# Gated delta stage of a streaming encoder step: front woven into the last gated unit, modulation loads issued after k times state, first-level blocks ahead of the state update

## The reference, cut to what matters

```python
# gated unit: y (tokens x 512) against w_glu (512 x 1024)
za, zb = jnp.split(y @ w_glu, 2, axis=-1)
y_a = za * jax.nn.sigmoid(zb)
# gated delta rule, 4 heads of 128, with the per-head decay and the write strength beta
A = strict_lower((k_beta @ k.T) * dmask);  T = inverse(eye + A)
v_new = u - w @ S                      # u, w = T @ (v_beta, k_beta * exp(decay))
o     = q_dec @ S + (q @ k.T * dmask) @ v_new
S     = S * exp(decay_last) + k_dec.T @ v_new
# modulation: six vectors of 1024 from the conditioning vector; the last four serve later stages
mod = silu(c) @ w_ada + b_ada          # w_ada is 1024 x 6144
```

## Time and profile before

| | us |
|---|---|
| runs of the kernel before (3) | 1420.83, 1422.02, 1426.58 |
| median | 1422.02 |
| the profiled execution: its own time | 1422.2 |
| its span in the trace | 1420.5 |
| gated delta stage in it, 408.7 to 594.1 | 185.4 |
| mean granted TensorE clock (1 is 2.4 GHz) | 0.98 |

### The profile page before, as it was taken

The page is one execution under the profiler, slowest core; times in us unless marked ns, Lnnn a source line. Parts: engine busy times, 40 slices in busy tenths (PEclk is TensorE's granted clock), DMA queues, the critical chain, the costliest instruction groups (busy, mean ns, idle before and its releaser), DMA issues.

```text
span 1420.5 us, 28873 instructions
## 1 busy us (share of the span) xinstructions
PE 1350.5 (95%) x10652; PEld 1237.5 (87%) x10652; DVE 952.9 (67%) x1487; ACT 584.7 (41%) x1331; POOL 547.7 (39%) x618
## 2 busy tenths in 40 slices
PE   5999899989989998899999999999999999999997
PEld 4899899988978887688799999999999997887675
DVE  6527686774367766687879655676666568676398
ACT  6524344436466564425544333333332325543120
POOL 4888866871122322133331434432443431000051
PEclk9999999999989999999999999999999999999999
DMA  9431435335455453432132444554344449996794
GB/s 345 125 103 47 113 94 134 104 88 151 113 179 164 140 177 128 147 116 82 67 105 95 131 162 146 186 186 157 124 160 157 149 153 378 379 332 219 261 328 180
DMA packets 184406, 234.61 MB, mean 165 GB/s; under 512 B 17709, under 2 KB 118641, under 8 KB 184305
## 3 DMA queue, kind: packets, MB, share of 16 engines
q1 hardware_dynamic: 180128, 221.36, 48.2%
q10 hardware_dynamic: 4176, 11.89, 2.2%
HBM read 170.29 MB, written 61.73 MB: 163 GB/s over the span
## 4 chain that ended last, share of the span: by engine, by line
PE 60%; DVE 7%; issue 4%; ACT 3%; POOL 1%; DMA 1%; POOLq 0%; ACTq 0%; DVEq 0%; SPq 0%
PE bank L2461 30%; PE bank L2375 12%; PE bank L308 3%; PE bank L1161 2%; PE bank L1745 2%; PE bank L1177 1%; PE bank L1175 1%; PE bank L2392 1%; ACT hp L1835 1%; DVE stat L1868 1%; PE bank L1225 1%; DVE xt L1903 1%; PE bank L1216 1%; PE bank L1206 1%; PE bank L1218 1%
## 5 line engine op out<-in xcount | busy, mean ns | idle before, releaser
L2375 PE MATMUL bank<-split 128*128 128x512 f32 x924 | 212.4, 390 | 3.3 <-DVE split L2508 3.0
L2375 PEld LDWEIGHTS bank<-split 128*128 128x128 f32 x924 | 172.6, 188 | 45.3 <-DVE split L2504 6.5
L2461 PE MATMUL bank<-Tlo,rh 128*128 128x272 f32 x640 | 184.7, 289 | 0.0
L2461 PE MATMUL bank<-Thi,rh 128*128 128x272 f32 x640 | 184.2, 288 | 0.0
L2461 PE MATMUL bank<-Thi,rl 128*128 128x272 f32 x640 | 184.0, 288 | 0.0
L308 PE MATMUL bank<-hT_hi,whi 128*128 128x384 f32 (+1 forms) x504 | 167.8, 333 | 3.5 <-DVE wlo L298 3.3
L308 PE MATMUL bank<-hT_hi,wlo 128*128 128x384 f32 (+1 forms) x504 | 165.8, 329 | 0.0
L308 PE MATMUL bank<-hT_lo,whi 128*128 128x384 f32 (+1 forms) x504 | 165.7, 329 | 0.0
L2461 PE MATMUL bank<-hT_lo,rh 128*128 128x272 f32 x480 | 138.5, 289 | 0.0
L2461 PE MATMUL bank<-hT_hi,rl 128*128 128x272 f32 x480 | 138.4, 288 | 0.0
L2461 PE MATMUL bank<-hT_hi,rh 128*128 128x272 f32 x480 | 137.9, 287 | 0.0
(11 more groups left out here) (443 smaller groups left out, 3329.8 us busy)
## 6 DMA issues: line engine op xcount, KB each, us to landing
wada<-w_ada SPq DMA_DIRECT2D x12, 2048.0 KB, 9.7
raw<-w_up SPq DMA_DIRECT2D x40, 512.0 KB, 5.0
wsum<-w_down SPq DMA_DIRECT2D x11, 1024.0 KB, 5.6
wt<-wsum SPq DMA_DIRECT2D x11, 1024.0 KB, 4.0
rW<-wt SPq DMA_DIRECT2D x44, 256.0 KB, 6.0
split<-split SPq DMA_DIRECT2D x22, 512.0 KB, 5.0
wraw<-w_in SPq DMA_DIRECT2D x21, 512.0 KB, 4.4
rows<-convrow ACTq DMA_DIRECT2D x16, 577.5 KB, 3.6
```

The lines of the kernel that those rows point to most:

```text
L2375: last = pe.matmul(ps[down_bank(q, r)][:], a[:, rows], w, start=(k == 0 and m == 0), stop=(k == KH - 1 and m == 2))
L2461: last = pe.matmul(ps[banks[c]][:, 0:NC], w[:, ks], a, start=(n < 3 and k == 0 and p == 0), stop=(k == 3 and p == 2), skip_group_check=True)
```

## The change

It has these parts, which all touch the stage's order and no arithmetic.

1. **Front.** The gate half of block 3 leaves `glu_pe` and is made in three pieces (`glu_gate`, banks 3, 4, 2) inside the delta stage's list; the transposes, products and ACT copies of tiles 0 and 1 stand between these pieces and those of the value half. Tile 0 has an Xc buffer of its own (`XcF`).
2. **Modulation loads.** `ada(t+2)` is issued behind k times state of tile t and behind the load of q, k, v, no longer at the end of pass t. `ada(1)` waits for level 4 of tile 0. The halves of the output weights (`wo_load`) move from the ends of passes 6 and 7 to behind k times state of passes 6 and 7.
3. **Modulation products.** `ada_rows` runs one pass earlier: `ada_rows(0)` in the front, `ada_rows(t+1)` at the end of pass t, none in pass 7. `ada_columns(t)` moves from behind `new_values` to ahead of `turn_v`, into free columns of bank 1, and only heads 2 and 3 of `outputs` wait for its reader.
4. **DVE.** `first_level(n)` goes ahead of `new_state(t)`. In pass 8 `wo_low(4)` and `tile_lo(0, 0)` go behind `new_state(8)`.
5. **ACT.** The exponentials of the decay go from behind the rounds to between the second and the third round.

```diff
 (gdn_loads)
             sp.wait_ge(on["glu_mix"], 12)
+            ada(0)
             qkv(2)
-            for t in range(2):
-                ada(t)
...
+            sp.wait_ge(on["g_X"], lvp(0, LV - 2, PAIRS - 1) + 1)
+            ada(1)
             for t in range(TILES):
-                if t == PTILES:
-                    sp.wait_ge(on["ada_mm"], ADA0 + PTILES)
-                    wo_load(1)
+                sp.wait_ge(on["g_kS"], (t + 1) * HEADS)
+                if t + 3 < TILES:
+                    sp.wait_ge(on["g_qd"], t + 1)
+                    qkv(t + 3)
+                if t + 2 < PTILES:
+                    sp.wait_ge(on["ada_mm"], ADA0 + t + 1)
+                    ada(t + 2)
+                if 1 <= t and t + 1 < TILES:
+                    sp.wait_ge(on["g_mix"], t)
+                    z(t + 1)
                 if t + 4 < TILES:
                     sp.wait_ge(on["g_E"], (t + 2) * 3 + 3)
                     decay_rows(t + 4)
...
-                if t == PTILES - 2:
+                if t in (PTILES - 2, PTILES - 1):
                     sp.wait_ge(on["ada_mm"], ADA0 + t + 1)
-                    wo_load(0)
+                    wo_load(t - (PTILES - 2))
 (gdn_pe, front)
+            glu_gate(pe, 0)
+            decay_turn(pe)
+            turn_k(0)
+            pe.wait_ge(on["gate_d"], 3)
+            turn_q(0, ALL)
+            glu_gate(pe, 1)
+            glu_gate(pe, 2)
+            gram(0, 0)
+            gram(0, 1)
             glu_last(pe, 0)
...
+            turn_k(1)
             glu_last(pe, 1)
+            pe.wait_ge(on["gates"], 1)
+            turn_A(0)
             glu_last(pe, 2)
             scores(0)
...
             level_X(0, 2)
+            ada_rows(0)
 (gdn_pe, pass)
                 if t:
                     turn_o(t - 1)
+                if t < PTILES:
+                    ada_columns(t)
                 if more:
                     turn_v(n, ALL)
                 new_values(t)
-                if t:
-                    ada_columns(t - 1)
                 outputs(t, FIRST2)
                 if more:
                     turn_A(n)
                 outputs(t, LAST2)
                 if more:
                     scores(n)
-                if t < PTILES:
-                    ada_rows(t)
+                if t + 1 < PTILES:
+                    ada_rows(t + 1)
 (outputs)
-                pe.wait_ge(on["mod_cols"], ADA0 + t)
+                if heads is LAST2:
+                    pe.wait_ge(on["mod_cols"], ADA0 + min(t + 1, PTILES))
 (gdn_act, pass)
                     if more:
-                        decay_diff(n, FIRST2)
+                        decay_diff(n, ALL)
                     keep_P(t, 4)
                     keep_P(t + 1, 1)
                     if more:
-                        decay_diff(n, LAST2)
+                        decay_exp(n)
+                        decay_row(n)
                     keep_P(t, 5)
                     keep_P(t + 1, 2)
                     whole_X(t)
                     if more:
-                        decay_exp(n)
-                        decay_row(n)
                         squares_k(n)
 (gdn_dve, pass)
-                else:
-                    wo_low(dve, 4)
-                    tile_lo(dve, 0, 0)
+                if more:
+                    first_level(n)
                 new_state(t)
                 if more:
-                    first_level(n)
                     later_levels(n)
...
                 else:
-                    dve.wait_ge(on["mod_st"][0], 32)
...
+                    wo_low(dve, 4)
+                    tile_lo(dve, 0, 0)
                     for k in range(5, KD):
                         wo_low(dve, k)
```

More of the change, by code:

```diff
@@ L946, in glu_act @@
                     gates_exp(act)
+            weights(3)
         def glu_dve(dve):
@@ L1170, in level_X @@
                         if l == LV - 1:
-                            last = pe.matmul(x_at(t, p, UP, i, 1), Pb[x][DOWN, h, 0:HB], Xc[x][DOWN, h, 1, :], start=True, stop=True)
+                            last = pe.matmul(x_at(t, p, UP, i, 1), Pb[x][DOWN, h, 0:HB], Xt(t)[DOWN, h, 1, :], start=True, stop=True)
                             continue
```

254 lines of the change are left out of this document (129 added, 125 removed).

## The result

The changed kernel takes **1402.47 us** (median of 4 runs, 1402.07 to 1403.87). The kernel before, measured beside it, took 1424.3 (4 runs, 1420.83 to 1427.94). The ratio is 0.9848, with a 95% interval from 0.9818 to 0.9878: faster by 1.2 to 1.8%. The profiled execution took 1402.45 with a span of 1400.7; before it was 1422.2 with 1420.5. The two profiles are 19.8 apart, and the sum had 13.2.

What follows compares the result with a forecast made beforehand. PE, busy 95%, bounds the kernel, so gains come from its stalls and waits in the delta stage. Terms -10.0, -3.0, -2.2, +2.1, -0.4, -1.0 and +1.3 sum to -13.2: 1422.2 to 1409.0 us, range 1402 to 1421.

Steps and rivals of the forecast that it cites:

- What bounds the kernel: PE busy 95% of the span; gains must come from its idle or slow time in the delta stage, not removed work.
- Loads: Delta passes 1 to 7: w_ada load moved behind k times state ends instruction-fetch stalls; -10.0 us, bounds 0 and -11.4.
- one stall that survives: Allowance of 1.4 us within the loads' saving, for one instruction-fetch gap remaining in the delta passes.
- The rival that the load is not the cause: PE's stalls in the delta passes have another cause, so the loads' saving falls away; 1419 us, chance 0.15.
- Columns: End of each delta pass: outputs no longer wait for DVE; -0.5 a pass, -3.0 for six, -2.2 for passes 7 and 8.
- First level ahead of the state: DVE at pass ends: state update finishes later and delays the next round; +0.3 a pass, +2.1 for seven passes.
- DVE becomes the bound: Rival: stalls go, but each delta pass pays the late state update and queued DVE work; 1416 us, chance 0.15.
- Exponentials: ACT's decay exponentials move to where ACT waits for PE in the rounds; taken as nothing, bounds -2 and 0.
- ada_rows earlier, passes 7 and 8: Pass 7 loses a 1.92 us PE product, but output-weight splits hold pass 8's first round; -0.4, bounds 0 and -1.9.
- Front: Ahead of pass 1: first coupling ready sooner, mostly given back by ACT's copies and added ada_rows(0); -1.0 us.
- Output projection: Two splits behind the last state update delay PE's first projection matmul by 2.4, partly hidden in idle time; +1.3 us.
- The slower rival: The load reaches the next delta pass's rounds, stalling every pass with lower clock, 3.9 us each; 1435 us, chance 0.07.

## Why the prediction was right, and where its sizes were off

**What bounds the kernel** held: PE's waits and clock in the delta stage, and not its work. The forecast's mechanism is what happened, and the three rivals fell. The number owes something to chance. The profiles are 19.8 apart where 13.2 was forecast, and the time came within 0.5 us of the range's end. Of the 19.8, 3.7 came with the clock in the front of before, and the stages ahead of the front took 1.8 of it back.

**Loads (-10.0 taken, of it -8.7 in passes 1 to 6).** Right in cause, a little small. Moving only the load gave -10.2 in these six passes, the full 10.1 that the bound held. That the fetches wait for the load, which the prediction had only from an overlap in time, is shown by the packets, which start 2.4 to 4.8 us later when the load stands ahead of the rounds. The term that was mis-sized is "one stall that survives", for which 1.4 was left: the one that did measured 0.59, and made its pass 1.0 longer than the gap-free ones beside it (20.50 against 19.53 and 19.52). In pass 7 the gap of 1.34 went as well in the changed kernel, though that pass's load is the output weights and the edit of w_ada alone did not remove it (1.61 there). The change moved the loads of the output weights too, which may be the reason; no run isolates it. The rival that the load is not the cause (1419) fell with both runs of the load. The Trainium skill, "Runtime: NRT & Kernel Launch", section "Instruction fetch mechanics", which stood beside this rival, calls a crossing "one DMA tail-bump, mostly hidden". The packets at 442, 462 and 482 us, met by a full q1 and followed by no gap, are as it says, while those in the rounds of short matmuls cost 0.97 to 1.70 each with the load put back. The rule holds here for the one place and not for the other.

**Columns (-0.5 a pass, between -0.15 and -1.1).** Right: 0.53 a pass by the run that undoes it. The outputs follow the new values after 1.18 (1.2 forecast). Of the 2.2 taken for passes 7 and 8 the half for pass 7 was wrong: with the columns put back that pass is as long (17.17), because its end waits for the state update behind the splits. The half for pass 8 can't be checked alone. With all other terms, the two passes gave -4.2 where -3.6 was forecast.

**First level ahead of the state (+2.1 for seven passes).** Wrong in size: 0.16 in passes 1 and 3, nothing in 2, 4 and 6, hidden in pass 5. The step that failed is the end of the state update, worked out at 536.6, which is 6.75 behind the outputs, where the next round started 6.03 behind them. It ended 6.08 behind them (503.68 against 497.60). The collision with POOL met one operation of the three and made it 1.41 instead of 0.42, so it was paid once and not carried on, and four heads took 1.11 and not 1.22. What was left is hidden where the round begins with the other tile, one in two as the prediction had said, and costs 0.16 where it does not. With this the rival "DVE becomes the bound" fell as well: none of passes 1 to 6 waits longer than these 0.16 for DVE's state or additions. The first round of pass 8 waits for a state update that the splits of the output weights hold. The wait is 1.89, and 1.1 of it went when the splits were moved.

**Exponentials (0).** Right, by the run that put them back.

**ada_rows earlier, passes 7 and 8 (-0.4).** Not isolated. The reason given, that the splits hold the first round of pass 8, is what the timeline shows, and moving them made passes 7 and 8 shorter by 1.9.

**Front (-1.0).** The pair of profiles says -3.7 at the start of pass 1, which is -5.5 in the front itself and +1.8 in stages that the change does not touch. What the prediction lacked is the clock: it looked at PE's two waits and not at the granted clock of the front of before (0.90 and 0.94), which alone made 3.7. At an equal clock the term is -1.75 by one profile, inside its bounds of -3.7 and +1.9 and larger than the -1.0 taken.

**Output projection (+1.3).** PE starts 2.4 behind the state update as worked out. What that costs stays open: the pair of profiles says 0, and the means over eight and three profiles say +1.3, with like profiles 2.4 apart. What the prediction did not see is what the chain of this stage hangs on. DVE's chain waits for POOL, and POOL for the row g1s: the two profiles with that load ahead have 134.5 and 134.3 in this stage, and the other eleven at least 135.8.

**The slower rival** (the stall moves along, 3.9 a pass) fell. The new load ends in the next pass's first round, and there is one gap of 0.59 in six passes.

**Sum for passes 1 to 6:** -10.2 for the load, -3.2 for the columns, +0.3 for the two rounds that wait and +1.0 for the pass with the surviving gap make -12.1, and the profile shows -12.7. The terms do not add to the tenth, since the load was moved alone in a kernel with the columns in their old place, and the columns were put back in one with the load in its new place. The last +0.8, in the 691 us behind the projection's stage, was not followed up; two profiles of the same kernel differ by more. The diff also moves the copy of the output rows on DVE behind the second round. The prediction did not mention it, and no run isolates it.

## What to carry to other kernels

Look for gaps with "issue" on PE beside large transfers, microsecond by microsecond, and put the transfer beside long matmuls instead of short ones: the move of one load was worth 10 us of 1422 without touching any arithmetic. Whether a gap is a fetch can be told by the instruction packet, which here landed 1.25 to 1.53 us before PE went on. Count a stretch from a matmul at its own start, and not from the start of the program, when two profiles are compared. Read the granted clock of every stretch before pricing what a reordering there will bring, since a lower clock can be most of a difference between two profiles. And before an engine's start is made earlier, follow the chain of its stage to the transfer that it hangs on; here that was a small row queued behind large ones.

## What the runs showed of the hardware that had not been expected

**A gap costs more than its length.** With the load at the start, five gaps of 6.4 us in all cost 8.3 against passes that held one of 0.6, and the gap of 0.59 made its pass 1.0 longer. In three kernels the clock fell after one: to 0.93 in pass 6 of before and in pass 2 with the load put back, and to 0.85 and 0.79 in passes 7 and 8 with only the load moved, which took 4.5 more than before. It did not fall after each gap. With the columns put back it fell to 0.50 in pass 8, behind 4 us in which PE was busy for 1.60; the wait there was for ACT's copy (1.74), so the fall follows idle time of either kind. It does not always come: in the old front 1.41 and 1.36 us busy of 4 were followed by 0.50, and 1.20 by 1.00.

**A fetch gap ends a fixed time behind its packet.** In 23 gaps, 0.24 to 2.30 us long, in twelve profiles, PE went on 1.25 to 1.53 us after the last 16 KB packet of q8 had landed. A load ahead of the packet made it start later by up to 4.8 us and left its own 0.9 to 1.4 us as they were.

**A full queue does not stall by itself.** Instruction packets that met q1 at 100 to 103% cost nothing between 442 and 483 us in the changed kernel, and one that met it at 54% was followed by 1.68 us of standstill in a round of short matmuls.

**A collision of DVE and POOL falls on whichever operation is there.** POOL's 1.27 us over 128x512 stretched the addition `Xc<-Xc,identc` from 0.42 to 1.41 in the changed kernel. In the one before it was the product `Lc<-ATc,maskc`, 1.14 beside POOL and 0.43 without it.
